# Four of the eight broadcast loads of a recurrence step issued from GpSimd's queue instead of SyncE's

## The reference

```
def step(state, inp):
    r_t, w_t, k_t, v_t, a_t, b_t = inp
    sa = jnp.einsum('bhvk,bhk->bhv', state, a_t)
    state = (state * w_t[:, :, None, :] + sa[..., None] * b_t[:, :, None, :]
             + v_t[..., None] * k_t[:, :, None, :])
    return state, jnp.einsum('bhvk,bhk->bhv', state, r_t)
...
_, out = lax.scan(step, s0, xs, reverse=reverse)
...
fwd = direction(dlo_f, glo_f, w0[0], w2[0], g2[0], False)
bwd = direction(dlo_b, glo_b, w0[1], w2[1], g2[1], True)
```

## Time and profile before

| | |
|---|---|
| median of three runs | 3304.49 us |
| the profiled execution | 3309.16 us, span of its instructions 3307.4 us |
| granted TensorE clock, mean over the span | 0.979 of full speed |
| PE busy | 3144.8 us (95%) |
| DVE busy | 2053.2 us (62%) |
| ACT busy | 1069.3 us (32%) |
| POOL busy | 309.2 us (9%) |
| recurrence with the attention beside it | about 540 to 1320 us of the span |
| store of the blocks, issue to landing | 1.5 us (median of 16) |
| a load `Dn<-nbs`, issue to landing | 2.9 to 7.7 us, median 5.3 us (128 loads) |
| VectorE's waits for these loads | 29.3 us in 11 of 16 steps |

### The profile page before, as it was taken

One profiled execution on the slowest core, in us unless ns is written; L12 is line 12 of the kernel. 1 busy time (PEld: TensorE's weight loads), 2 busy tenths in 40 slices (PEclk: granted clock), 3 DMA queues, 4 the chain that ended last, 5 costly groups with the idle time before them and its releaser, 6 DMA issues.

```text
span 3307.4 us, 51994 instructions
## 1 busy us (share of the span) xinstructions
PE 3144.8 (95%) x21948; PEld 2518.0 (76%) x21948; DVE 2053.2 (62%) x3255; ACT 1069.3 (32%) x1528; POOL 309.2 (9%) x303
## 2 busy tenths in 40 slices
PE   8998997888898888999999999999999999999999
PEld 7787885677666667778888888877746888778887
DVE  6665554577777776545444544449979987655444
ACT  5222334444445443222111111132153333433332
POOL 0322441000000001301000000000000000000000
PEclk9999999899999999999999999999999999999999
DMA  4333666234344433421111111111101222223222
GB/s 149 128 131 98 220 209 188 71 87 110 77 98 101 100 75 140 147 89 51 51 40 51 51 51 51 40 38 51 39 13 61 93 102 91 88 88 117 101 89 77
DMA packets 93527, 301.86 MB, mean 91 GB/s; under 512 B 10352, under 2 KB 38640, under 8 KB 70768
## 3 DMA queue, kind: packets, MB, share of 16 engines
q1 hardware_dynamic: 79104, 246.63, 24.1%
q0 software_dynamic: 14192, 51.91, 4.5%
HBM read 241.35 MB, written 57.15 MB: 90 GB/s over the span
## 4 chain that ended last, share of the span: by engine, by line
PE 78%; DVE 12%; issue 3%; DMA 3%; ACT 2%; POOL 1%; SPq 1%; DVEq 0%; ACTq 0%; POOLq 0%
PE ps L2444 26%; PE ps L308 21%; PE ps L490 7%; PE ps L1747 3%; PE ps L2250 2%; PE ps L2587 2%; PE ps L1758 1%; PE ps L2066 1%; DMA Dn<-nbs 1%; DVE Yh L2614 1%; PE ps L1770 1%; PE ps L1009 1%; PE ps L1415 1%; PE ps L2464 1%; DVE pr L1591 1%
## 5 line engine op out<-in xcount | busy, mean ns | idle before, releaser
L2444 PE MATMUL ps<-Hh,whi 128*128 128x512 f32 x1600 | 497.7, 392 | 0.6 <-DVE wlo L288 0.6
L284 ACT ACTIVATE whi<-raw 128x2048 fp32r<-128x2048 f32 x139 | 265.6, 1911 | 520.3 <-PE ps L308 296.4
L288 DVE TENSOR_TENSOR wlo<-raw,whi 128x2048 fp32r<-128x2048 f32 x139 | 319.0, 2295 | 96.0 <-ACT whi L284 95.8
L2444 PEld LDWEIGHTS ps<-Hh,whi 128*128 128x128 f32 x1600 | 300.1, 188 | 69.5 <-issue 5.8
L2444 PE MATMUL ps<-Hh,wlo 128*128 128x512 f32 x800 | 311.3, 389 | 0.0
L308 PE MATMUL ps<-Hhi,whi 128*128 128x512 f32 x672 | 206.9, 389 | 0.0
L308 PE MATMUL ps<-Hhi,wlo 128*128 128x512 f32 x672 | 206.9, 389 | 0.0
L308 PE MATMUL ps<-Hlo,whi 128*128 128x512 f32 x672 | 206.9, 389 | 0.0
L2444 PE MATMUL ps<-aHh,whi 128*128 128x512 f32 x512 | 199.3, 389 | 0.1
L2444 PE MATMUL ps<-aHh,wlo 128*128 128x512 f32 x512 | 199.2, 389 | 0.0
L2444 PE MATMUL ps<-aLh,whi 128*128 128x512 f32 x512 | 199.2, 389 | 0.0
(11 more groups left out here) (383 smaller groups left out, 6123.0 us busy)
## 6 DMA issues: line engine op xcount, KB each, us to landing
raw<-in_panels SPq DMA_DIRECT2D x139, 1024.0 KB, 4.8
rwf<-F POOLq DMA_DIRECT2D x16, 1280.0 KB, 6.6
L<-rwf SPq DMA_DIRECT2D x16, 1024.0 KB, 5.0
L<-rwf SPq DMA_DIRECT2D x64, 256.0 KB, 3.9
Dn<-nbs SPq DMA_DIRECT2D x128, 128.0 KB, 5.3
gts<-so POOLq DMA_DIRECT2D x16, 512.0 KB, 4.0
gl<-gts SPq DMA_DIRECT2D x32, 256.0 KB, 3.4
rwt<-so POOLq DMA_DIRECT2D x15, 512.0 KB, 2.9
```

Of the source, the lines that this page charges most:

```text
L284: e.activation(whi[i % 2][:, :], raw_of(i)[:, :], AF.Copy).then_inc(*a_hi.up(i))
L288: e.tensor_tensor(wlo[i % 2][:, :], raw_of(i)[:, :], whi[i % 2][:, :].bitcast(F32), OP.subtract).then_inc(*v_lo.up(i))
L2444: m = e.matmul(ap, W[wi][:, kc, n0:n0 + 128], mov[mi][:, kc, :], start=x == 0 and q == 0, stop=x == len(kcs) - 1 and q == 2)
```

## The change

The four loads q = 0 to 3 stay in SyncE's call `Nc`. The four loads q = 4 to 7 move to a new call `Nc` of GpSimd, which first waits for the same two things as SyncE: the landing of the store, and the second half of the scores' matmuls (`SC`, 1). GpSimd's loads have landing semaphores of their own, four for each direction (`d_np`), and the group `d_n` shrinks from nine to five. VectorE's wait ahead of `row0` takes q = 0 to 3 from the one group and q = 4 to 7 from the other. What a load reads and writes is the same.

```diff
-    d_l, d_g, d_n, d_ob = (... for x, n in (("d_l", 3), ("d_g", 2), ("d_n", 9), ("d_ob", 1)))
+    d_l, d_g, d_n, d_ob = (... for x, n in (("d_l", 3), ("d_g", 2), ("d_n", 5), ("d_ob", 1)))
+    d_np = [landings(f"d_np{d}", 4) for d in range(2)]
...
                 for q in range(8):
-                    e.wait_ge(*d_n[d].by(s, q))
+                    e.wait_ge(*(d_n if q < 4 else d_np)[d].by(s, q))
...
+        if c == "Nc":
+            e.wait_ge(*d_n[d].by(s, "st"))
+            e.wait_ge(*t_w[d].by(s, "SC", 1))
+            for q in range(4, 8):
+                blocks(e, x, nbs[d, s % 2], q, d_np[d], s)
...
+    def blocks(e, x, nb, q, landing, s):
+
+        e.dma_start(x.Dn[16 * q:16 * (q + 1), :], nb[16 * q:16 * (q + 1), :].rearrange("u f -> (u f)")[None, :]
+                    .broadcast_to([16, 2048])).then_inc(*landing.up(s, q))
...
             e.wait_ge(*t_w[d].by(s, "SC", 1))
-            for q in range(8):
-                e.dma_start(x.Dn[16 * q:16 * (q + 1), :], nb[16 * q:16 * (q + 1), :].rearrange("u f -> (u f)")[None, :]
-                            .broadcast_to([16, 2048])).then_inc(*d_n[d].up(s, q))
+            for q in range(4):
+                blocks(e, x, nb, q, d_n[d], s)
```

More of the change, by code:

```diff
@@ L1217, in build @@
     t_w, v_w, a_w, g_w = ([signals(f"{x}_w{d}") for d in range(2)] for x in "tvag")
-    d_l, d_g, d_n, d_ob = ([landings(f"{x}{d}", n) for d in range(2)] for x, n in (("d_l", 3), ("d_g", 2), ("d_n", 9), ("d_ob", 1)))
+    d_l, d_g, d_n, d_ob = ([landings(f"{x}{d}", n) for d in range(2)] for x, n in (("d_l", 3), ("d_g", 2), ("d_n", 5), ("d_ob", 1)))
+    d_np = [landings(f"d_np{d}", 4) for d in range(2)]
     d_lng = landings("d_lng", 1)
```

## The result

| | before | after |
|---|---|---|
| median, timed in turn on one chip | 3307.84 us (4 runs) | 3346.86 us (4 runs, 3342.95 to 3356.77) |
| ratio to before | 1 | 1.0113, 95% interval 1.0091 to 1.0136 |
| span of the profiled execution | 3307.4 us | 3343.4 us |
| granted TensorE clock over the span | 0.979 | 0.974 |

The change costs 1.13%, or 36 us of span. The forecast was no change, with 3320 us as its upper end. So it was wrong. To a loss of over 0.5% it had given a chance of 0.12, to a gain of that size 0.10.

The account below looks back on a forecast made before the run. No engine was full; work moves at the pace of whichever engine is late, with VectorE waiting 29.3 us for Dn. A gain of 11 x 0.3 = 3.3 us (0.1%) gave 3301.5 us, 8-in-10 range 3286 to 3320 us.

Parts of the forecast that it names:

- The claim that the transfers set the landing: At the Dn loads: landings come 1.07 us apart, issues 0.45 us apart, so transfers, not SyncE's issue, set the landing.
- Step 4: Transfers of the eight 128 KB pieces: last landing gains 0.3 us per step, within -0.3 and +0.9.
- the forecast's own sign of being wrong: Dn loads: last landing moves by more than 1 us either way, or moves and the time does not follow.
- Rival A: Dn transfers: the two halves run side by side, landing 2.5 to 4.3 us sooner; 3283 to 3288 us, chance 0.16.
- rival B: GpSimd's loads: each held up 1.8 us while VectorE is busy, landing 1.5 us late; 3321 to 3329 us, chance 0.14.
- Rival C: Wait of row0: SyncE's later loads crowd in before GpSimd's last piece; 11 to 13 us lost, 3315 us, chance 0.08.
- The sum: Over the 11 steps where VectorE waits for Dn: 11 x 0.3 = 3.3 us gained, 0.1%, giving 3301.5 us.
- Step 1: SyncE's list: four loads fewer free it 1.8 us earlier; Qb, Kp, Pv and L issue sooner, counted as 0.
- step 3: GpSimd's list: its new wait ahead of the loads delays nothing behind it that matters; cost 0.
- no engine is full: Stretch 550 to 1260: TensorE busy 607.5 of 710 us, VectorE 505.7, GpSimd 51.7; whichever engine is late sets the pace.

Follow-up runs that it names:

- experiment 1: Against the changed kernel, all eight loads of a step come from GpSimd's queue and none from SyncE's: 3312.97 us, 1.0017 of the kernel before.
- experiment 6: Against the changed kernel, GpSimd's four loads in turn, issued only when SyncE's fourth has landed: 3343.63 us, 1.0103 of the kernel before.
- experiment 7: Against the changed kernel, GpSimd issues only one load (q = 7) and SyncE the other seven: 0.9989 of the kernel before.
- experiment 4: Against the changed kernel, 128 already fulfilled waits stand ahead of TensorE's part, shifting its instruction list: 1.0143 of the kernel before.
- with two loads: Against the changed kernel, GpSimd issues two of the eight loads (q = 6 and 7) and SyncE six: 1.0057 of the kernel before.
- one load on 8 engines: Against the kernel before, one SyncE load for all 128 partitions replaces the eight for 16 partitions each: 3342.32 us, 1.0100.
- four small loads: Against the kernel before, blocks stored twice and loaded for all 128 partitions in four loads by column quarter (2 KB pieces): 3287.02 us, 0.9933.
- one-load version of the blocks stored twice: Against the kernel before, blocks stored twice and read by one load for all 128 partitions over 16 DMA engines: 3302.83 us, 0.9987.
- experiment 12: Against the version with blocks stored twice and four column-quarter loads, two of the four are issued from GpSimd's queue: 3290.69 us, 0.9932 of the kernel before.
- ScalarE's version: Against the changed kernel, the wait and the four loads q = 4 to 7 stand in ScalarE's list instead of GpSimd's: 3381.06 us, 1.0214 of the kernel before.

## Why the prediction was wrong

**What held.** The claim that the transfers set the landing held at the median (issues in 1.7 and 1.9 us, last landing at 10.45 us instead of 10.28). Step 4, on the transfers, was sized at a gain of 0.3 us for each step within -0.3 and +0.9. Eight of 16 steps lie outside on the losing side, and the forecast's own sign of being wrong, a landing moved by over 1 us, came in the ninth and fourteenth step. The waits that it acts on went up by 3.5 us, to 32.8, instead of down by 3.3, so its sign was off; but this is a tenth of the loss. Rival A (two halves side by side) did not occur: the first two waits grew. Of rival B (GpSimd's loads start late) one sign came, 7.8 us to land for GpSimd's four, and the other did not: VectorE waits in 11 steps as before. Its mechanism did not occur: GpSimd issues 0.49 us apart, and all eight on it cost 0.17%. The end of B's range, 3321 to 3329 us, lies nearest to the result, and that is luck: the reason isn't B's. Rival C, SyncE's later loads crowding in, is there in the fifth and ninth step, where `Kp` and `Vp` follow at once and the last landing comes 0.9 and 2.65 us later. VectorE does not wait for the loads in these two, so what C counted, a later product, did not cost there.

**What failed.** The sum had no term for TensorE: what the transfers do to TensorE was put at nothing without a reason, and it measured 25.5 us of added stalls and 12.2 us of slower matmuls. Steps 1 and 3 of the change part by part are where it is missing. Step 1 asked what stands behind the loads in SyncE's list, and step 3 what stands behind them in GpSimd's. Neither asked who else uses the DMA engines at that moment, and the answer is TensorE's own instruction stream. Step 4 did weigh two queues served in turn, but for the loads alone. The rows were in the trace of the kernel before. TensorE's idle time of 10.1 us in five places without a releaser at L1415 was the sign, with 1.23 us of it in the fifth step, in which the forecast counted the loads as hidden because VectorE did not wait for them. And "no engine is full" was read from the average of 607.5 of 710 us. In the forward steps VectorE waits for the group that the fetch interrupts (L1415 has 4.6% of the chain in the earlier trace rows), so what delays TensorE there can reach the end.

**What was missing, in size.** Stalls 25.5 us, of which experiments 1, 6 and 7 show the condition (two queues with several loads in flight at once, for 18.5 us of it; in the fifth and ninth step it can be `Kp` and `Vp` issued sooner) and 4 the place (the fetch, not the operation). Then 12.2 us of slower matmuls. Each of the stalls over 3 us goes with a stretch at 0.50, but so do other waits, and how much of the 12.2 us each brings was not told apart. The table supports this account in the main: stalls plus busy plus waits changed by +41.3 us against a recurrence of +35.1 after, +22.3 against +17.8 with two loads, +39.5 against +35.7 in turn, +35.7 against +32.4 with one load on 8 engines, -21.5 against -14.5 with four small loads. It fits less well for the one-load version of the blocks stored twice (-8.8 against -1.4) and for experiment 12 (-4.0 against +1.8). ScalarE's version doesn't fit (+46.7 against +65.3); its own waits may come on top.

**What stays open.** Why a second queue delays the fetch by as much as 4.8 us. In the six steps it starts only 0.1 to 1.3 us before the last of the eight loads has landed. The Trainium skill, "DMA: Bandwidth & Descriptors", section "Queues, rings and completion order", says that a DMA engine takes turns between its queues, packet by packet. By that rule a second queue puts one more packet ahead of the fetch in each turn. That gives the direction. If such a packet is one piece of a load, it takes about 1.0 us (the median of GpSimd's pieces in the fifth step), and the delays measured in the six steps are 2.4 to 4.8 us; if it holds several pieces, the size could fit too. No run here separates the two. Nor was it tried to put the fetch at another place relative to the loads in single steps, or to hold SyncE's later loads at their old place, which would part their share from the second queue's in the fifth and ninth step.

## What to carry to other kernels

A second issuing queue sped up nothing here, where the transfers were the limit, and it can hold up the instruction fetch of an engine that runs many small instructions meanwhile. Look for idle time with no releaser on such an engine, ask what the DMA engines carry just ahead of it, and count the drop of the clock after a long stall as a second cost. If the loads themselves are slow for their size, change their shape first: all 16 DMA engines and small pieces gave 0.67% here, where two queues cost 1.13%. And look at the sizes of the packets after a change of queue: GpSimd's queue moved pieces of 2 KB as packets of 4 KB.

## What the runs showed of the hardware

- The instruction fetch of TensorE is a DMA among the data's, and it is held up by them. A 16 KB packet took 0.9 to 1.75 us before and after, and where TensorE stalled it went on 1.15 to 2.0 us after its end. The Trainium skill, "Runtime: NRT & Kernel Launch", section "Instruction fetch mechanics", calls the cost of such a block mostly hidden. By count that holds here: of the 83 fetches in the recurrence 77 before and 71 after brought no stall over 0.9 us. The others brought 11.9 us before and 37.4 us after.
- The Trainium skill, "DMA: Bandwidth & Descriptors", section "Issuing engines are not separate DMA queues", says that issuing from several engines saves only the issue time. The landing agrees at the median (10.28 against 10.45 us). The time does not: it rose by 1.13% with four loads on GpSimd.
- A broadcast load in pieces of 8 KB moved one piece in 0.61 us on each of 8 engines when it was one DMA, and as loads of one piece on each of 16 engines the landings were 1.03 us apart at the median. Stored twice, the 1 MB landed in 7.2 us (median) instead of some 10.3 us.
- Loads in pieces of 2 KB went as 128 packets of 4 KB for 512 KB on GpSimd's queue, and as 256 packets of 2 KB on SyncE's (experiment 12).
- GpSimd issued these DMAs 0.49 us apart, against 0.60 us in the row that the prediction used.
